# Stage one on rows of x that also come in turned, latents normalised out of PSUM, and a reordered down ring

## Chip, core and metric

One core of a Trainium2 chip runs the whole layer. The metric is the device time of one execution in microseconds. The engines are TensorE (PE, matmuls; PEld is its weight load), VectorE (DVE), ScalarE (ACT), GpSimd (POOL) and SyncE (SP, which here only queues transfers).

## What is computed

One layer on x (1024 x 1024, fp32), shortened:

```python
z = rmsnorm(x, mix_norm_g) @ w_in               # heads of retention, then 448 columns of latents
c_q, c_kv, k_pe = last 448 columns of z         # 256, 128, 64
ret = retention(...)                            # 4 heads
att = mla(rmsnorm(c_q), rmsnorm(c_kv), k_pe)    # 4 heads
x = x + concat(ret, att) @ w_o
h = rmsnorm(x, ffn_norm_g)
x = x + (silu(h @ w_gate) * (h @ w_up)) @ w_down
x = x + sigmoid(rmsnorm(x, ple_norm_g) @ w_ple_gate) * (p @ w_ple_proj)
return rmsnorm(x, final_norm_g)
```

## The kernel before

Each engine runs a program written out by hand; order is kept by semaphores. A full-precision product is three matmuls: every operand is split into a high part (a copy on ScalarE, `..._hi`) and a low part (a subtraction, `..._lo`, on VectorE or POOL), and `product` adds high x high, high x low, low x high over K = 8 slices, 24 matmuls.

Stage one (`sp_1`, `pool_1`, `act_1`, `dve_1`, `pe_1`) makes the latents, tile by tile (T = 8 tiles of 128 tokens). TensorE turns the rows of x (`norm_turn`, L232, 8 transposes), one tile ahead of the product; ScalarE and VectorE split the turned tile out of PSUM (L242, L249) and the weight slices (`mixed_hi` L179, `mixed_lo` L182; the norm's gain is in the weights); ScalarE takes the squares of x (L211) and in `latent_out` the squares of the latents (L335, L336) and their copy, scaled by the row's rstd (L338); VectorE then normalises them in place (`latent_rows`, L413). Two banks of PSUM take the products in turn. The weights of the first retention head come in and are split meanwhile; the angle tables of the rotation are made at tiles 2 and 3. Retention (`pe_2`) starts when all eight copies are done (`ckv_out`).

The down projection's ring (`pe_step`, L1893 to L1895) is one level of a Strassen-like scheme: five chunks of seven steps (35 in all), each 4 x 6 matmuls on a stationary part (hidden rows from DRAM, `sp_rows`, low part by POOL in `rows_lo`, L1871) and a moving part (`w_ffn_down`, `sp_moving`, high part L1859, low part by VectorE in `ring_lo`, L1866). Four of the seven moving parts, T1 to T4, are differences that POOL makes (`moving_sum`: L1833, L1837, L1840, L1845) from four 128 x 1024 slots raw(0) to raw(3). VectorE's program for step s is: two adds of the product to x (L1282), ring_lo of step s+3, two adds. A step may write a bank when the add of an earlier step is done (one to four steps back). SP's program is in one line too: for each u the rows of step u, then moving loads and every four steps a piece of the next stage's weights (`sp_piece`, which waits until the piece before it is split; VectorE splits pieces 2 to 5 between the steps, L182). After the ring `pe_down` (L1936 to L1938) does the last two row blocks with parts made by `down_hi` and `down_lo` (L1920). Stage six turns p on TensorE, two transposes for each of eight tiles (L2237).

## Time and profile before

| | us |
|---|---|
| median of 3 runs | 1295.79 (1295.27 to 1299.84) |
| profiled execution | 1300.8, its span 1299.0 |
| TensorE busy | 1253.7 (97%) |
| VectorE busy | 714.4 (55%) |
| ScalarE busy | 482.7 (37%) |
| GpSimd busy | 486.0 (37%) |

Spans count from the first instruction. A row of a time line has the start, the length, the engine, the line of the kernel, the operation, out<-in, the shape and how many were merged; in brackets the idle time of the engine before it and what ended that. Matmuls overlap, so their pace is the distance of their starts, not their length.

### The profile page before, as it was taken

To read this page: it belongs to the slowest core of one execution; us is meant where nothing else is said; L and a number is where in the kernel's file an instruction comes from. 1 tells how busy PE (TensorE), PEld (TensorE's weight loads), DVE (VectorE), ACT (ScalarE), POOL (GpSimd) and SP (SyncE) were. 2 spreads that over 40 slices of the span, in tenths; PEclk is the share of its full clock that TensorE was granted. 3 is DMA by queue.
4 is the path that set the end of the run, shared out by engine and by line. 5 is a ranking of instruction groups with operands and counts; after the bars stand their busy time and mean duration, and the time that the engine had idled before them with its cause. 6 is when DMAs were issued, how large, how long until landed. Compare 5 with 4: busy or idle time off the path is not lost.

```text
span 1299.0 us, 16923 instructions
## 1 busy us (share of the span) xinstructions
PE 1253.7 (97%) x6052; PEld 1052.9 (81%) x6052; DVE 714.4 (55%) x1193; ACT 482.7 (37%) x889; POOL 486.0 (37%) x502
## 2 busy tenths in 40 slices
PE   7999999989998999999999999999999999999997
PEld 6888888877888888878888888888888778778886
DVE  4634444467556326754444555444489888754433
ACT  5732222246666114533333333333343334314422
POOL 2334444441000002374334555433478777610001
PEclk9999999999999999999999999999999989999999
DMA  6411111010011400133323332332454464330002
GB/s 209 133 34 49 33 50 33 1 41 1 1 65 66 146 1 1 46 109 122 112 83 90 122 111 92 122 102 80 159 212 138 136 211 146 117 110 1 1 33 98
DMA packets 101692, 110.90 MB, mean 85 GB/s; under 512 B 4848, under 2 KB 68720, under 8 KB 101616
## 3 DMA queue, kind: packets, MB, share of 16 engines
q1 hardware_dynamic: 101328, 109.38, 25.8%
q8 instruction: 46, 0.75, 0.2%
q10 hardware_dynamic: 288, 0.52, 0.1%
q14 instruction: 30, 0.25, 0.1%
HBM read 86.29 MB, written 23.59 MB: 85 GB/s over the span
## 4 chain that ended last, share of the span: by engine, by line
PE 74%; issue 9%; POOL 9%; DVE 3%; DMA 2%; ACT 2%; SPq 0%; POOLq 0%; ACTq 0%; DVEq 0%
PE PS L1561 10%; PE PS L1562 10%; PE PS L1563 10%; PE PS L204 4%; PE PS L206 4%; PE PS L205 4%; PE PS L913 3%; PE PS L1893 3%; PE PS L1895 3%; PE PS L1894 3%; PE PS L929 3%; PE PS L2247 2%; PE PS L2245 2%; PE PS L2246 2%; PE PS L708 2%
## 5 line engine op out<-in xcount | busy, mean ns | idle before, releaser
L204 PE MATMUL PS<-WF,HTH 128*128 128x512 f32 (+1 forms) x448 | 177.6, 396 | 2.2 <-ACT X L338 1.5
L206 PE MATMUL PS<-WF,HTL 128*128 128x512 f32 (+1 forms) x448 | 174.0, 388 | 0.0
L205 PE MATMUL PS<-WF,HTH 128*128 128x512 f32 (+1 forms) x448 | 173.7, 388 | 0.0
L1282 DVE TENSOR_TENSOR X<-X,PS 128x512 f32<-128x512 f32 x172 | 110.9, 679 | 79.0 <-PE PS L206 52.7
L1561 PE MATMUL PS<-HTH,WF 128*128 128x512 f32 x336 | 130.7, 389 | 0.0
L1562 PE MATMUL PS<-HTL,WF 128*128 128x512 f32 x336 | 130.7, 389 | 0.0
L1563 PE MATMUL PS<-HTH,WF 128*128 128x512 f32 x336 | 130.7, 389 | 0.0
L1494 DVE TENSOR_TENSOR WF<-RAW,WF 128x512 fp32r<-128x512 f32 x63 | 69.6, 1106 | 81.5 <-ACT WF L1484 81.5
L1561 PE MATMUL PS<-WF 128*128 128x512 f32 x252 | 98.7, 392 | 2.0 <-issue 2.0
L204 PEld LDWEIGHTS PS<-WF,HTH 128*128 128x128 f32 x448 | 84.8, 189 | 17.6 <-ACT X L338 1.9
L1563 PE MATMUL PS<-WF 128*128 128x512 f32 x252 | 98.8, 392 | 0.0
L1562 PE MATMUL PS<-WF 128*128 128x512 f32 x252 | 98.7, 392 | 0.0
L206 PEld LDWEIGHTS PS<-WF,HTL 128*128 128x128 f32 x448 | 84.5, 189 | 16.3
L205 PEld LDWEIGHTS PS<-WF,HTH 128*128 128x128 f32 x448 | 84.8, 189 | 14.9
L1893 PE MATMUL PS<-HTH 128*128 128x512 f32 x200 | 77.8, 389 | 0.0
L1894 PE MATMUL PS<-HTL,HTH 128*128 128x512 f32 x200 | 77.8, 389 | 0.0
L1895 PE MATMUL PS<-HTH,HTL 128*128 128x512 f32 x200 | 77.8, 389 | 0.0
L217 POOL TENSOR_SCALAR ST<-ST 128x1 f32<-128x1 f32 x24 | 5.3, 223 | 189.7 <-ACT HTH L1274 112.6
L561 ACT ACTIVATE TMP<-PS,ST 128x384 f32<-128x384 f32 x32 | 18.6, 580 | 152.5 <-PE PS L206 152.5
L1702 POOL TENSOR_TENSOR TMP<-TMP 128x512 f32<-128x512 f32 x10 | 16.1, 1606 | 157.4 <-DVE TMP L1686 157.4
L1563 PEld LDWEIGHTS PS<-HTH,WF 128*128 128x128 f32 x336 | 63.1, 188 | 13.2
L1561 PEld LDWEIGHTS PS<-HTH,WF 128*128 128x128 f32 x336 | 63.1, 188 | 13.1
(248 smaller groups left out, 2857.6 us busy)
## 6 DMA issues: line engine op xcount, KB each, us to landing
hid<-TMP SPq DMA_DIRECT2D x74, 256.0 KB, 2.3
TMP<-hid SPq DMA_DIRECT2D x25, 512.0 KB, 4.1
RAW<-in_w_ffn_gate SPq DMA_DIRECT2D x22, 512.0 KB, 4.2
RAW<-in_w_ffn_up SPq DMA_DIRECT2D x22, 512.0 KB, 5.5
RAW<-in_w_ffn_down SPq DMA_DIRECT2D x22, 512.0 KB, 5.4
X<-in_x SPq DMA_DIRECT2D x16, 512.0 KB, 4.5
RAW<-in_w_in SPq DMA_DIRECT2D x32, 256.0 KB, 3.2
TAB<-hid SPq DMA_DIRECT2D x9, 512.0 KB, 4.7
```

Of the source, the lines that this page charges most:

```text
L204: nc.tensor.matmul(dst, HTH[:, k, tok], w_h, start=(k == 0), stop=False)
L205: nc.tensor.matmul(dst, HTH[:, k, tok], w_l, start=False, stop=False)
L206: last = nc.tensor.matmul(dst, HTL[:, k, tok], w_h, start=False, stop=(k == K - 1))
L913: last = nc.tensor.matmul(dst, a[:, tok], b[:, blk], start=(i == 0), stop=(i == 4))
L1282: nc.vector.tensor_tensor(x, x, src, ALU.add).then_inc(done, 1)
L1494: nc.vector.tensor_tensor(part(name, 1), part_raw(j, name), part(name, 0).bitcast(F32), ALU.subtract).then_inc(f_w_lo, 1)
L1561: nc.tensor.matmul(dst, w_h, m_h, start=(first and k == 0), stop=False, skip_group_check=True)
L1562: nc.tensor.matmul(dst, w_h, m_l, start=False, stop=False, skip_group_check=True)
L1563: last = nc.tensor.matmul(dst, w_l, m_h, start=False, stop=(k == 3), skip_group_check=True)
L1893: nc.tensor.matmul(dst, h_h, w_h, start=(q < 3 and k == 0), stop=False, skip_group_check=True)
L1894: nc.tensor.matmul(dst, h_h, w_l, start=False, stop=False, skip_group_check=True)
L1895: last = nc.tensor.matmul(dst, h_l, w_h, start=False, stop=(k == 1), skip_group_check=True)
```

## The change

x is also passed in turned (`x_turned`, per tile 128 x 8 x 128), so stage one has no transposes; x itself still comes in, for the squares. Turned tiles lie in six places of X and TMP. The transfer order on SP is new, with the first head's weights in it. All gains come in one load from ScalarE's queue. ScalarE runs one small activation first. TensorE runs 18 products of zeros first. The first weight slices are signalled by halves. Latents stay in PSUM (four banks) until VectorE has scaled and normalised them from there; POOL multiplies the two rstds. The angle tables are at tiles 6 and 7. Retention's first four products wait for the bank they use.

In the ring the moving loads are queued two steps earlier, in another order, and the pieces two steps later; T1 is made in raw(0) instead of T_BUF, after B11's low part, and T2 one step earlier. The four low parts for `pe_down` are made before the last step's adds, in the order 0, 3, 1, 2 (`LAST_ORDER`). p is passed in turned too, and is split from SBUF.

The diff without unchanged and minor lines (eight columns of indent are cut; `...` is what is left out):

```diff
@@ -250,44 +252,82 @@
...
+TURNED_AT = (2048, 3072, 6144, 7168, None, 2048, 3072, None)
+def rows_turned(t):
+    a = TURNED_AT[t]
+    x = tmp(2048, 1024) if a is None else X[:, a:a + 1024]
+    return x.rearrange("p (k n) -> p k n", k=K)
 def sp_1(e):
-    e.dma_start(X3[:, 0, :], t_in["x"][0:P, :]).then_inc(s_x[0], 16)
-    e.dma_start(ident, t_in["table"][:, C_IDENT:C_IDENT + P]).then_inc(s_ident, 16)
-    e.dma_start(GK[:, 0:K], t_in["mix_gain"]).then_inc(s_gk, 16)
-    e.dma_start(GK[:, 2 * K:3 * K], t_in["ple_gain"]).then_inc(s_gk, 16)
     w = t_in["w_in"].rearrange("(k p) n -> p k n", p=P)
-    for m in range(4):
+    def turned(t):
+        if t >= 4:
+            e.wait_ge(s_e[t % 4], 16)
+        if t >= 5:
+            e.wait_ge(n_mix.lo, 10 if t == 7 else 2 * (t - 5) + 2)
+        e.dma_start(rows_turned(t), t_in["x_turned"][t]).then_inc(s_e[t % 4], 16)
+    def rows(t):
+        if t >= 2:
+            e.wait_ge(n_mix.squares, t - 1)
+        e.dma_start(X3[:, t % 2, :], t_in["x"][t * P:(t + 1) * P, :]).then_inc(s_x[t % 4], 16)
+    def weights(m):
...
                     w[:, 2 * m:2 * m + 2, 4 * HALF:4 * HALF + MLA_IN]).then_inc(s_raw[m % 4], 16)
-    for t in range(1, 4):
-        e.dma_start(X3[:, t, :], t_in["x"][t * P:(t + 1) * P, :]).then_inc(s_x[t], 16)
+    turned(0)
+    for m in range(3):
+        weights(m)
+    turned(1)
+    weights(3)
+    rows(0)
+    turned(2)
+    rows(1)
+    turned(3)
...
     e.dma_start(GC[:, QL:QL + KVL], t_in["kv_norm_g"].partition_broadcast(P)).then_inc(s_const, 16)
-    for t in range(4, T):
-        e.wait_ge(n_mix.turned, t - 3)
-        e.wait_ge(n_mix.squares, t - 3)
-        e.dma_start(X3[:, t % 4, :], t_in["x"][t * P:(t + 1) * P, :]).then_inc(s_x[t % 4], 16)
+    turned(4)
+    rows(2)
+    sp_head_weights(e, 0, 0)
+    turned(5)
+    sp_head_weights(e, 0, 1)
+    rows(3)
+    turned(6)
+    sp_head_weights(e, 0, 2)
+    sp_head_weights(e, 0, 3)
+    rows(4)
+    turned(7)
+    rows(5)
+    rows(6)
+    rows(7)
+    e.dma_start(ident, t_in["table"][:, C_IDENT:C_IDENT + P]).then_inc(s_ident, 16)
+IDLE = tmp(3072, P)
 def pool_setup(e):
+    nc.gpsimd.memset(IDLE, 0.0).then_inc(s_setup, 1)
...
     nc.gpsimd.memset(GNE[:, :], GN_EPS).then_inc(s_setup, 1)
-    nc.gpsimd.memset(GK[:, K:2 * K], 1.0).then_inc(s_setup, 1)
...
 def pool_1(e):
...
     def latent_rstd(t):
-        e.wait_ge(ckv_out, 3 * t + 2)
+        e.wait_ge(ckv_out, 2 * t + 2)
...
         e.wait_ge(lat_mean, 2 * t + 2)
-        nc.gpsimd.tensor_tensor(ST[:, 32 + 2 * t:34 + 2 * t], ST[:, 16 + 2 * t:18 + 2 * t], NEGH[:, 0:2],
-                                ALU.pow).then_inc(lat_rstd, 1)
+        c = ST[:, 32 + 2 * t:34 + 2 * t]
+        nc.gpsimd.tensor_tensor(c, ST[:, 16 + 2 * t:18 + 2 * t], NEGH[:, 0:2], ALU.pow).then_inc(lat_rstd, 1)
+        e.wait_ge(lat_rstd, 2 * t + 1)
+        nc.gpsimd.tensor_tensor(c, c, rstd_of(0, t).to_broadcast([P, 2]), ALU.mult).then_inc(lat_rstd, 1)
...
@@ -301,41 +341,57 @@
...
             e.wait_ge(n_mix.squares, t)
-        norm_squares(e, n_mix, t, 0, X3[:, t % 4, :], tmp(0, 1024))
-    e.wait_ge(s_gk, 32)
-    for c in range(4):
+        norm_squares(e, n_mix, t, 0, X3[:, t % 2, :], tmp(0, 1024))
+    def high(t, k=0, n=K):
+        e.wait_ge(s_e[t % 4], 16 * (t // 4 + 1))
+        d = slice(t * P, t * P + P)
+        nc.scalar.copy(HTH[:, k:k + n, d], rows_turned(t)[:, k:k + n]).then_inc(n_mix.hi, n // 4)
+    def slices(c):
         arrived(e, c)
-        mixed_hi(GK, 0, c, raw(c), MLA_IN)
-        if c == 0:
-            turned_hi(e, n_mix, 0)
-    squares(0)
+        for i in range(2):
+            a = c * 1024 + i * HALF
+            gained_hi(WF[:, a:a + MLA_IN], raw(c)[:, i * MLA_IN:(i + 1) * MLA_IN],
+                      GK[:, 2 * c + i:2 * c + i + 1]).then_inc(w_hi if i else w_even_hi, 1)
+    e.dma_start(GK[:, :], t_in["gains"]).then_inc(s_gk, 16)
+    e.wait_ge(s_setup, 4)
+    nc.scalar.activation(ST[:, 120:121], PIH[:, 0:1], ACT.Square).then_inc(s_warm, 1)
+    e.wait_ge(s_gk, 16)
+    high(0, 0, 4)
+    slices(0)
+    high(0, 4, 4)
+    slices(1)
+    slices(2)
+    high(1)
+    slices(3)
     for t in range(T):
-        if t + 1 < T:
-            turned_hi(e, n_mix, t + 1)
-            squares(t + 1)
+        if t + 2 < T:
+            high(t + 2)
+        squares(t)
         if t >= 1:
-            latent_out(e, t - 1)
-        if t >= 4:
-            arrived(e, M_RET + t - 4)
-            e.wait_ge(s_rawb[t - 4], 16)
-            mixed_hi(GK, 1, t - 4, raw(t))
-        if t == 3:
+            latent_squares(e, t - 1)
+        if 3 <= t <= 6:
+            c = t - 3
+            arrived(e, M_RET + c)
+            e.wait_ge(s_rawb[c], 16)
+            mixed_hi(GK, 1, c, raw(c))
+        if t == 7:
...
     e.dma_start(QDEC, t_in["query_decay"]).then_inc(s_const, 16)
-    latent_out(e, T - 1)
-def latent_out(e, t):
+    latent_squares(e, T - 1)
+def latent_squares(e, t):
     e.wait_ge(lat_done, t + 1)
-    b = PS[:, 4 + t % 2]
+    b = PS[:, 4 + t % 4]
     if t:
-        e.wait_ge(ckv_out, 3 * t)
+        e.wait_ge(ckv_out, 2 * t)
...
                          accum_out=ST[:, 17 + 2 * t:18 + 2 * t]).then_inc(ckv_out, 1)
-    nc.scalar.activation(CKV[:, t, 0:MLA_IN], b[:, 0:MLA_IN], ACT.Copy, scale=r).then_inc(ckv_out, 1)
...
@@ -372,26 +428,42 @@
...
 def dve_1(e):
-    def weights_lo(g, c, n=HALF):
-        m = g * M_RET + c
-        e.wait_ge(w_hi, m + 1)
-        mixed_lo(GK, g, c, raw(m), n)
-    for c in range(4):
-        weights_lo(0, c, MLA_IN)
-        if c == 0:
-            turned_lo(e, n_mix, 0)
+    def weights_lo(c):
+        e.wait_ge(w_hi, M_RET + c + 1)
+        mixed_lo(GK, 1, c, raw(c))
+    def low(t, k=0, n=K):
+        e.wait_ge(n_mix.hi, 2 * t + (k + n) // 4)
+        d = slice(t * P, t * P + P)
+        nc.vector.tensor_tensor(HTL[:, k:k + n, d], rows_turned(t)[:, k:k + n], HTH[:, k:k + n, d].bitcast(F32),
+                                ALU.subtract).then_inc(n_mix.lo, n // 4)
+    def slices(c):
+        for i in range(2):
+            a = c * 1024 + i * HALF
+            e.wait_ge(w_hi if i else w_even_hi, c + 1)
+            gained_lo(WF[:, a + 4096:a + 4096 + MLA_IN], raw(c)[:, i * MLA_IN:(i + 1) * MLA_IN],
+                      WF[:, a:a + MLA_IN], GK[:, 2 * c + i:2 * c + i + 1]).then_inc(w_lo if i else w_even_lo, 1)
+    low(0, 0, 4)
+    slices(0)
+    low(0, 4, 4)
+    slices(1)
+    slices(2)
+    low(1)
+    slices(3)
     for t in range(T):
-        if t + 1 < T:
-            turned_lo(e, n_mix, t + 1)
-        if t >= 4:
-            weights_lo(1, t - 4)
-        if t == 2:
+        if t + 2 < T:
+            low(t + 2)
+        if 3 <= t <= 6:
+            weights_lo(t - 3)
+        if t >= 2:
+            latent_rows(e, t - 2)
+        if t == 6:
             tables_dve(e)
-        if t >= 3:
-            latent_rows(e, t - 3)
-    for t in range(T - 3, T):
+    for t in range(T - 2, T):
...
+    e.wait_ge(lat_rows, 3 * T)
...
@@ -406,28 +478,33 @@
 def latent_rows(e, t):
-    e.wait_ge(lat_rstd, t + 1)
-    e.wait_ge(ckv_out, 3 * t + 3)
-    for n, (a, b) in enumerate(((0, QL), (QL, QL + KVL))):
-        c = CKV[:, t, a:b]
-        nc.vector.scalar_tensor_tensor(c, c, ST[:, 32 + 2 * t + n:33 + 2 * t + n], GC[:, a:b],
-                                       ALU.mult, ALU.mult).then_inc(lat_rows, 1)
+    b = PS[:, 4 + t % 4]
+    e.wait_ge(n_mix.rstd, 2 * t + 2)
+    e.wait_ge(ckv_out, 2 * t + 2)
+    nc.vector.tensor_scalar(CKV[:, t, QL + KVL:MLA_IN], b[:, QL + KVL:MLA_IN], rstd_of(0, t), None,
+                            ALU.mult).then_inc(lat_rows, 1)
+    e.wait_ge(lat_rstd, 2 * t + 2)
+    for n, (a, b_end) in enumerate(((0, QL), (QL, QL + KVL))):
+        nc.vector.scalar_tensor_tensor(CKV[:, t, a:b_end], b[:, a:b_end], ST[:, 32 + 2 * t + n:33 + 2 * t + n],
+                                       GC[:, a:b_end], ALU.mult, ALU.mult).then_inc(lat_rows, 1)
+def idle_products(n):
+    for _ in range(n):
+        nc.tensor.matmul(bank(7, P), IDLE, IDLE, start=True, stop=True)
 def pe_1(e):
-    e.wait_ge(s_ident, 16)
-    def turn(t):
-        e.wait_ge(s_x[t % 4], 16 * (t // 4 + 1))
-        norm_turn(e, n_mix, t, X3[:, t % 4, :])
-    turn(0)
+    e.wait_ge(s_setup, 1)
+    idle_products(18)
+    def first(k):
+        if k == 4:
+            e.wait_ge(n_mix.lo, 2)
+        e.wait_ge(w_lo if k % 2 else w_even_lo, k // 2 + 1)
     for t in range(T):
-        if t + 1 < T:
-            turn(t + 1)
-        e.wait_ge(n_mix.lo, 2 * t + 2)
-        if t >= 2:
-            e.wait_ge(ckv_out, 3 * (t - 1))
-        product(bank(4 + t % 2, MLA_IN), t, 0, MLA_IN,
-                (lambda k: e.wait_ge(w_lo, k // 2 + 1)) if t == 0 else None).then_inc(lat_done, 1)
+        e.wait_ge(n_mix.lo, 2 * t + 2 if t else 1)
+        if t >= 4:
+            e.wait_ge(lat_rows, 3 * (t - 3))
+        product(bank(4 + t % 4, MLA_IN), t, 0, MLA_IN, first if t == 0 else None).then_inc(lat_done, 1)
...
@@ -452,15 +529,17 @@
...
+def sp_head_weights(e, h, c):
+    w = t_in["w_in"][:, 0:4 * HALF].rearrange("(k p) (s c) -> p k s c", p=P, s=4)
+    e.wait_ge(w_lo, 4 * h + c + 1)
+    for k in range(2):
+        e.dma_start(RAW[:, c * 1024 + k * HALF:c * 1024 + (k + 1) * HALF].rearrange("p (s c) -> p s c", s=4),
+                    w[:, 2 * c + k, :, h * HD:(h + 1) * HD]).then_inc((s_rawb if k else s_raw)[c], 16)
 def sp_retention(e):
-    w = t_in["w_in"][:, 0:4 * HALF].rearrange("(k p) (s c) -> p k s c", p=P, s=4)
-    with e.Fori(0, HEADS) as h:
+    for h in range(1, HEADS):
         for c in range(4):
-            e.wait_ge(w_lo, M_RET + c - 3 + 4 * h)
-            for k in range(2):
-                e.dma_start(RAW[:, c * 1024 + k * HALF:c * 1024 + (k + 1) * HALF].rearrange("p (s c) -> p s c", s=4),
-                            w[:, 2 * c + k, :, bass.ds(h * HD, HD)]).then_inc((s_rawb if k else s_raw)[c], 16)
+            sp_head_weights(e, h, c)
...
@@ -507,8 +586,10 @@
...
 def pe_2(e):
-    e.wait_ge(ckv_out, 3 * T)
+    e.wait_ge(s_ident, 16)
     for s in range(NR + 3):
+        if s < 4:
+            e.wait_ge(lat_rows, 3 * (5 + s))
...
@@ -1513,15 +1594,15 @@
...
         c, q = u // 7, u % 7
+        if u >= 14 and u % 4 == 2:
+            sp_piece(e, (u - 14) // 4)
...
             sp_moving(e, c + 1, (0,))
-        if c and q == 2:
-            sp_moving(e, c, (1, 3))
-        if c and q == 3:
+        if c and q == 0:
+            sp_moving(e, c, (3, 1))
+        if c and q == 1:
             sp_moving(e, c, (2,))
-        if u >= 12 and u % 4 == 0:
-            sp_piece(e, u // 4 - 3)
-    sp_moving(e, CHUNKS, (1, 3, 2))
+    sp_moving(e, CHUNKS, (3, 1, 2))
...
@@ -1719,13 +1800,14 @@
...
             moving_sum(e, c, 0)
-        if q in (3, 4, 5):
-            moving_sum(e, c, q - 2)
+        if q in MOVING_SUM_AT:
+            moving_sum(e, c, MOVING_SUM_AT[q])
...
+MOVING_SUM_AT = {2: 1, 4: 2, 5: 3}
...
@@ -1775,7 +1857,7 @@
...
         return raw({"B11": 0, "B21": 1, "B22": 3}[name])
-    return raw(2) if name == "T3" else T_BUF
+    return {"T1": raw(0), "T3": raw(2)}.get(name, T_BUF)
...
@@ -1798,8 +1880,8 @@
...
         if c and g == 0:
-            e.wait_ge(r_t, 4 * c - 3)
-            e.wait_ge(d_lo, 7 * c - 6)
+            e.wait_ge(r_t, 4 * c - 2)
+            e.wait_ge(d_lo, 7 * c - 4)
...
@@ -1824,17 +1906,18 @@
 def moving_sum(e, c, n):
     if n == 0:
+        moving_arrived(e, c, 0)
+        moving_arrived(e, c, 2)
+        e.wait_ge(d_lo, 7 * c + 1)
+        nc.gpsimd.tensor_tensor(raw(0), raw(2), raw(0), ALU.subtract).then_inc(r_t, 1)
+    if n == 1:
...
             e.wait_ge(d_lo, 7 * c)
-        moving_arrived(e, c, 0)
-        moving_arrived(e, c, 2)
-        nc.gpsimd.tensor_tensor(T_BUF, raw(2), raw(0), ALU.subtract).then_inc(r_t, 1)
-    if n == 1:
         moving_arrived(e, c, 3)
-        e.wait_ge(d_lo, 7 * c + 3)
-        nc.gpsimd.tensor_tensor(T_BUF, raw(3), T_BUF, ALU.subtract).then_inc(r_t, 1)
+        e.wait_ge(r_t, 4 * c + 1)
+        nc.gpsimd.tensor_tensor(T_BUF, raw(3), raw(0), ALU.subtract).then_inc(r_t, 1)
...
@@ -1926,7 +2011,7 @@
...
             if n < 4:
-                e.wait_ge(f_added, N_DOWN - 2 + n if n < 2 else N_DOWN)
+                e.wait_ge(f_added, N_DOWN - 1 if n == 0 else N_DOWN)
...
@@ -1976,22 +2061,24 @@
...
             ring_lo(e, s + 3)
+        elif s < STEPS - 1:
+            down_lo(e, LAST_ORDER[s + 3 - STEPS])
...
             piece_lo(e, (s - 10) // 4)
-        if s >= 31:
-            down_lo(e, s - 31)
-s_p, p_turned, p_hi, p_lo = sem("s_p"), sem("p_turned"), sem("p_hi"), sem("p_lo")
-s_e = [sem(f"s_e{i}") for i in range(4)]
+        if s == STEPS - 2:
+            down_lo(e, LAST_ORDER[2])
+            down_lo(e, LAST_ORDER[3])
+s_p, p_hi, p_lo = sem("s_p"), sem("p_hi"), sem("p_lo")
...
 PW = 16384
-PIN = tmp(0, 2048).rearrange("p (t n) -> p t n", t=T)
+PIN = tmp(0, 2048).rearrange("p (k n) -> p k n", k=2)
...
@@ -2085,15 +2172,15 @@
 def p_part(t, y):
...
-def p_bank(t):
-    return PS[:, 5 + 2 * (t % 2), 0:2 * P].rearrange("p (k n) -> p k n", k=2)
+def p_rows(t):
+    return PIN[:, :, t * P:t * P + P]
 def act_6(e):
     def p_high(t):
-        e.wait_ge(p_turned, t + 1)
         if t == 0:
+            e.wait_ge(s_p, 16)
             e.wait_ge(f_down, N_DOWN + 2 * T)
-        nc.scalar.copy(p_part(t, 0), p_bank(t)).then_inc(p_hi, 1)
+        nc.scalar.copy(p_part(t, 0), p_rows(t)).then_inc(p_hi, 1)
...
@@ -2233,9 +2319,6 @@
...
         if half == 0:
-            for k in range(2):
-                last = nc.tensor.transpose(PS[:, 5 + 2 * (u % 2), k * P:k * P + P], PIN[:, t, k * P:k * P + P], ident)
-            last.then_inc(p_turned, 1)
...
```

## Rows read from the trace of the kernel before

**Rows 1.** The page, first part: busy time, share of the span, instructions.
```profile
PE 1253.7 (97%) x6052; PEld 1052.9 (81%) x6052; DVE 714.4 (55%) x1193; ACT 482.7 (37%) x889; POOL 486.0 (37%) x502
```
**Rows 2.** TensorE's waits, whole span: who waited for whom, us, times, longest.
```profile
PE PS L1893 <- DVE X L1282: 7.1, 3, 3.0
...
PE PS L1936 <- DVE WF L1920: 1.9, 1, 1.9
```
**Rows 3.** Time line of TensorE in stage one.
```profile
11.71 1.97 PE L232 MATMUL PS<-CST,X 128*128 128x128 f32 x8 [5.13 <-DMA X<-in_x]
13.33 0.72 PE L204 MATMUL PS<-WF,HTH 128*128 128x448 f32 x1
...
20.05 1.03 PE L232 MATMUL PS<-CST,X 128*128 128x128 f32 x8
20.84 0.45 PE L204 MATMUL PS<-WF,HTH 128*128 128x448 f32 x1
...
25.79 1.03 PE L232 MATMUL PS<-CST,X 128*128 128x128 f32 x8
...
61.04 0.50 PE L204 MATMUL PS<-WF,HTH 128*128 128x512 f32 x1 [1.53 <-ACT X L338]
```
**Rows 4.** Time lines of SP, ScalarE and VectorE at the front.
```profile
2.59 1.97 SPq L260 DMA_DIRECT2D RAW<-in_w_in  x4
...
6.94 1.28 ACT L179 ACT_TABLE_LOAD   x1 [6.94 <-DMA RAW<-in_w_in]
...
11.89 3.66 DVE L182 SCALAR_TENSOR_TENSOR WF<-RAW,GK,WF 128x448 fp32r<-128x448 f32 x6
```
**Rows 5.** The tile RAW, first 16 us: its four loads.
```profile
DMA to landing us min/median/max: 4.3/5.3/6.3
```
**Rows 6.** Stretches: length, busy PE, PEld, DVE, ACT, POOL, clock, DMA share, GB/s.
```profile
12.00:14.00 2.00, 2.00 (x10) 1.96 (x9) 2.00 (x4) 2.00 (x5) 0.00 (x0) 1.00 1.01 398
...
45.00:50.00 5.00, 5.00 (x30) 4.65 (x29) 2.83 (x6) 3.93 (x11) 1.82 (x5) 1.00 0.38 108
```
**Rows 7.** VectorE by line and form in the ring: busy us, mean ns.
```profile
L1920 DVE TENSOR_TENSOR WF<-RAW,WF 128x1024 fp32r<-128x1024 f32 x4 | 4.9, 1215 | 0.0
```
**Rows 8.** The ring as one stretch.
```profile
944.64:1150.20 205.56, 196.46 (x841) 160.22 (x840) 174.63 (x186) 73.75 (x78) 146.73 (x54) 0.98 0.45 156
```
**Rows 9.** Time line of TensorE in the ring.
```profile
982.90 0.39 PE L1893 MATMUL PS<-HTH 128*128 128x512 f32 x1
...
988.35 0.39 PE L1893 MATMUL PS<-WF 128*128 128x512 f32 x1
...
1036.64 0.50 PE L1893 MATMUL PS<-WF 128*128 128x512 f32 x1 [1.44 <-DVE X L1282]
...
1058.95 0.77 PE L1893 MATMUL PS<-WF 128*128 128x512 f32 x1 [2.96 <-DVE X L1282]
...
1063.78 0.63 PE L1895 MATMUL PS<-WF 128*128 128x512 f32 x1
...
1108.31 0.47 PE L1893 MATMUL PS<-WF 128*128 128x512 f32 x1 [2.72 <-DVE X L1282]
...
1150.20 0.71 PE L1936 MATMUL PS<-WF 128*128 128x512 f32 x1 [1.91 <-DVE WF L1920]
```
**Rows 10.** Waits of POOL and of SP's queue in the ring.
```profile
POOL TMP L1833 <- DMA RAW<-in_w_ffn_down: 22.5, 4, 6.8
...
SPq L2054 <- DVE WF L182: 34.1, 3, 15.7
```
**Rows 11.** Time lines of POOL and VectorE in the ring.
```profile
1032.52 2.39 POOL L1840 TENSOR_TENSOR RAW<-RAW 128x1024 f32<-128x1024 f32 x1
1032.59 3.40 DVE L1866 TENSOR_TENSOR HTL<-RAW,HTH 128x1024 fp32r<-128x1024 f32 x1
...
1041.61 2.47 DVE L1282 TENSOR_TENSOR X<-X,PS 128x512 f32<-128x512 f32 x4
```
**Rows 12.** TensorE by line and form, stage six.
```profile
L2237 PE MATMUL PS<-CST,TMP 128*128 128x128 f32 x16 | 3.0, 272 | 0.0
```

27 lines of the change are left out of this document (16 added, 11 removed).

## The prediction

> **What bounds the kernel now.** I read the page's first part, then TensorE's waits, then time lines of the two places where these waits lie. TensorE's matmuls are busy for 97% of the span [rows 1], so time can come only from fewer instructions on TensorE, from its waits, or from stretches at half clock. The longest sums of waits are in the down stage: 7.1 us at L1893 for adds on VectorE, and 1.9 us at L1936 [rows 2]. The other place is the front. The second block of transposes waits 5.13 us for x, the first product starts at 13.33, and retention starts at 61.04 after a last wait of 1.53 us for ScalarE's copy of the latents [rows 3].
>
> The profiled execution took 1300.8 us for a span of 1299.0, 5.0 us over the median of 1295.79. The sum is made against the former; at the end I come back to the difference.
>
> **Part 1, the front.** Product 0 ends at 20.05; behind it come seven products of 4.95 us (20.84 to 25.79), 34.6 in all, and six blocks of eight transposes at 0.79 us (20.05 to 20.84), 4.7 in all, so product 7 ends at 59.4, and 1.7 us with the wait of 1.53 in them lie before 61.04 [rows 3]. Stage one's transposes go, since rows of x come in turned. This takes 6 x 0.79 = 4.7 us off the path, and the wait for the copy (1.7 us) goes too: retention's first product needs only the latents of tile 4, out of a bank that was done 3 products before.
>
> What is left is the start of product 1: 20.84 before. Now it comes when the low part of the last weight slice is there. Loads: before, x's first rows, three small loads and the first weights, 1.06 MB, had landed at 2.59 + 4.3 = 6.9 us, the last weights at about 4.1 + 6.3 = 10.4; the rate with a full queue is 398 GB/s [rows 4 to 6]. After, only turned tile 0 stands ahead of the weights, at 1.18 instead of 2.59. I place the first slice at 5.8 (between 5.4, if the 0.46 MB follow the first load at 398 GB/s, and 6.8), each next at +1.2, the last at 10.7 with turned tile 1 between. The table load of 1.28 us that ScalarE did after the first landing [rows 4] is brought forward by the warm-up activation and hidden by the load. VectorE is the slow one: half-slice of weights 0.61 (3.66 us for six [rows 4]), a turned tile 1.2 (as the 1024 columns at L1920, 1215 ns [rows 7]). From 6.4, when ScalarE has its first half: eight half-slices 4.9, the second half of tile 0 0.6, tile 1 1.2, half a microsecond of gaps: the last is done at 13.4 and the product at 14.0 us. Seven products without transposes, 7 x 4.90 = 34.3, end at 48.3. So retention starts at 48.3 instead of 61.04: **-12.7 us**. The range is -9.5 (loads at the late bound, no ScalarE lead, half clock through product 0 and 1) to -14.
>
> What hides the rest: ScalarE per tile does a copy, squares, latent squares and a weight pair; it was busy 3.93 of 5 us with the latent copy in it, which goes [rows 6]. VectorE gets three reads of PSUM per tile in place of two of SBUF; it has 2.83 of 5 us [rows 6]. Four banks in turn instead of two give these reads three products of room. SP now queues 11.2 MB before turned tile 7; at 398 GB/s that is done at about 31 us, and product 7 needs it at 43. rows(t) waits for the squares of t-2, and turned tiles, head weights stand behind it on SP, but tiles are asked for two products ahead. The angle tables move to tile 6 on VectorE (nine operations), and behind them the last latents wait, so VectorE comes to retention's first tile about when TensorE has finished the second projection: 0 to 2 us of new wait there; I take 0.
>
> The 18 zero products are costed at nothing: eight transposes at 0.23 us apart (11.71, x8, 1.97 us [rows 3]) make about 4 us for 18, which end before the weights are there. Their worth is the clock: product 0 took 6.72 us (13.33 to 20.05) against 4.95 for a later one, since its first ten matmuls ran at the 1.2 GHz spacing; after, it is paced by VectorE anyway, so a clock that stays low costs 0.5 us, bounds 0 and 2.
>
> **Part 2, the down ring.** 35 steps took 205.56 us (944.64 to 1150.20); an undisturbed step is 5.45 (982.90 to 988.35), 35 of them 190.7. So 14.9 us are lost: 1.44 + 2.96 + 2.72 + 1.91 us of waits, and 5.9 around them, most of it half clock: behind the waits of 2.96 and of 2.72 matmuls start 0.43 apart instead of 0.23 (row at 1063.78) [rows 8, 9]. The last wait (1.91) also lowers the clock in the part behind the ring: another 1.6, priced like the row at 1108.31.
>
> Cause: POOL waits 22.5 us for moving rows in four chunk starts, and SP stood 34.1 us at the piece loads waiting for VectorE [rows 10], with the moving and row loads queued behind. POOL's sums come late, ScalarE and ring_lo behind them, and the adds stand behind ring_lo in VectorE's program. The change asks for the moving rows two steps earlier, and for the pieces two later, when the buffer is nearly free; T2 is a step earlier too. T1 now goes into the slot of B11 and waits for B11's low part, which VectorE does at step 7c-3; ring_lo of T1 is due at 7c-1, two steps or 10.9 us later, against 2.4 for the sum and 1.05 for the copy. POOL then waits for VectorE there, with rows_lo of the next steps queued behind, but they are due later still. So I expect the DMA waits to go and nothing as long in their place. At the end the four low parts come before the last step's adds instead of one behind them, so the 1.91 goes as well. I leave 1.5 us of small waits: -14.9 - 1.6 + 1.5 = **-15.0 us**, range -17 to -7.
>
> What speaks against it: VectorE's SBUF reads collide with POOL. A low part takes 1.2 us alone [rows 7] but 3.40 beside POOL's sum at 1032.52 (2.39). With four adds in a row (2.47 [rows 11]) that makes 5.7 to 5.9 a step, more than TensorE's 5.45; POOL's waits were what let VectorE catch up. POOL needs 11 x 2.39 a chunk, two per such cycle, so 5.5 of 7 steps are of the long kind and the chunk takes VectorE 37 of 38.1 us; in the chunk with three pieces it overruns by some 3 us, against 4 us of room before an add is late.
> The Trainium skill (SBUF — State Buffer, "SBUF: two separate sides") says the pair of ports that VectorE and GpSimd share is an exclusive lock, and that an operation with two SBUF inputs blocks fully against one of GpSimd that reads SBUF; the rows agree (1.2 plus a whole 2.4 is 3.6), and by that rule a POOL that never waits is no free gain but takes VectorE over the step, which is rival 1.
>
> **Part 3, p.** p comes in turned: 16 transposes of stage six go. At 0.11 us apart (eight in 0.79 with the change-over [rows 3]; x16, 272 ns each with the pipeline [rows 12]) that is **-1.8 us**. The splits now read SBUF instead of PSUM, and have no due time before the gate product's 24 matmuls end.
>
> Sum: -12.7 - 15.0 - 1.8 = -29.5; 1300.8 - 29.5 = 1271.3. Against the median of 1295.79 it would be 1266.3. Part of the 5.0 between them is probably waits and half clock of the ring, which go anyway; I take the middle: **1268.5 us**.
>
> **Rivals.**
> 1. The ring becomes bound by VectorE and POOL's shared port: 35 steps of 5.71 us (1.21 + two POOL operations of 2.39 less overlap) are 199.9, 9.2 over the ideal. For it: 3.40 at 1032.59. Against: POOL needs only 11 of 14 places. Time 1268.5 + 7.7 = 1276.
> 2. The ring keeps its loss, with POOL waiting for B11's low part instead of the DMA: 1268.5 + 15.0 = 1283.5. Against: the 10.9 us of room.
> 3. The front gains only the transposes (the slices come as late as before): 1268.5 + 6.5 = 1275.
> 4. Slower: x now comes in twice, and stage one waits for its loads. It decides if the 11.2 MB take longer than 43 us; to lose all, retention would have to start 16.8 us later than before, turned tile 7 at 73, a rate under 160 GB/s. At 140 it is 1305. Against it 398 GB/s [rows 6].
> 5. The order on SP does not do what it says: pieces still block. Then as 2.
>
> **Numbers.** Chances: forecast 0.66, rival 1 0.15, rivals 2 and 5 0.07, rival 3 0.09, rival 4 0.03. The range goes from 1260 (both parts at their good ends) to 1284, which takes in rivals 1 to 3. A measurement of this kernel can tell about 0.5%, 6.5 us, from no change; every case but the fourth gains more, so faster 0.95, same 0.03, slower 0.02.
>
> **What would show it.** Right: product 1 at 14 us, no transposes up to the first head, retention at 48; POOL's wait at T1 no longer for a DMA; the ring 192 to 194 us, no half clock in it; the down part starting under 0.3 us after the ring. Wrong: a wait for x's turned rows in stage one; ring steps of 5.7; a wait for low parts of T1; TensorE waiting for VectorE just after the first retention product.

## The result, and the profile after

The changed kernel takes 1276.19 us (median of four runs, 1275.8 to 1279.47) against 1296.69 for the kernel before, run beside it: a ratio of 0.9843, 95% interval 0.9823 to 0.9863, 20.5 us less. The forecast of 1268.5 was 27.3 under the median of before that it knew (1295.79), so the changed kernel came in 7.7 over it and inside the range of 1260 to 1284. The profiled execution took 1279.47 us, with a span of 1277.7, 21.3 less than before's 1299.0. The readings below are of that execution. A granted clock of 1.00 is TensorE's full 2.4 GHz, 0.50 is the half clock of 1.2 GHz, and a value between is the mean of a stretch that has both.

The page's first part, which answers to [rows 1], and TensorE's waits over the whole span (engine and line that waits, who is waited for, us, times, longest), which answer to [rows 2]:

```profile
PE 1245.1 (97%) x6008; PEld 1046.6 (82%) x6008; DVE 730.6 (57%) x1194; ACT 480.3 (38%) x875; POOL 495.1 (39%) x510
```

```profile
PE PS L994 <- ACT TMP L1035: 4.2, 4, 1.1
PE PS L1976 <- DVE X L1363: 3.4, 4, 1.5
PE PS L1642 <- issue: 2.9, 1, 2.9
...
PE PS L607 <- POOL TMP L673: 2.1, 2, 1.9
```

The ring's waits for adds (L1976 for L1363, in before L1893 for L1282) fell from 7.1 to 3.4 us, and the wait behind the ring is gone. A new one stands at L607: 1.9 us for POOL, in the first head of retention.

The time line of TensorE in stage one, which answers to [rows 3] (start, length, engine and line, operation, idle time before it and its releaser):

```profile
12.80 0.47 PE L206 MATMUL PS<-WF,HTH 128*128 128x448 f32 x1 [0.95 <-DVE WF L184]
...
14.13 0.37 PE L206 MATMUL PS<-WF,HTH 128*128 128x448 f32 x1
...
48.65 0.39 PE L206 MATMUL PS<-WF,HTH 128*128 128x512 f32 x1
...
61.60 0.36 PE L607 MATMUL PS<-CST,TMP 128*128 128x128 f32 x1 [1.89 <-POOL TMP L673]
61.83 0.78 PE L206 MATMUL PS<-WF,HTH 128*128 128x512 f32 x1
```

Product 1 starts at 14.13 in place of 20.84, held up by the low parts of the weights, and retention at 48.65 in place of 61.04. Then comes the wait, and the matmul behind it takes 0.78 us in place of 0.39. The stretches of the changed kernel (length, busy us of PE, PEld, DVE, ACT, POOL, granted clock, DMA share, GB/s): ten microseconds with that wait in them, the ring, the part up to the gate stage, and the rest.

```profile
60.00:70.00 10.00, 8.40 (x33) 6.88 (x34) 2.50 (x5) 1.79 (x6) 3.27 (x6) 0.83 0.19 53
...
937.25:1132.43 195.18, 191.79 (x841) 157.31 (x840) 188.38 (x186) 74.57 (x78) 150.34 (x54) 1.00 0.49 166
1132.43:1156.81 24.38, 24.38 (x122) 20.42 (x120) 12.69 (x19) 9.01 (x16) 5.20 (x14) 1.00 0.26 100
1156.81:1277.70 120.89, 113.62 (x523) 94.14 (x521) 49.01 (x73) 39.39 (x82) 8.26 (x19) 0.98 0.09 35
```

So the span's 21.3 us divide as follows. Retention starts 12.4 earlier; 5.0 of that are lost again by the ring's start (944.64 to 937.25, 7.4 ahead), 3.6 of them within three products of retention. The ring is 10.4 shorter [rows 8], at full clock throughout. The part behind it is 1.9 shorter (26.32 to 24.38), and the rest 1.6 (122.5 to 120.9).

What is left in the ring, on TensorE (answering to [rows 9]), on VectorE and among POOL's waits there (answering to [rows 10]):

```profile
1047.63 0.47 PE L1976 MATMUL PS<-WF 128*128 128x512 f32 x1 [1.42 <-DVE X L1363]
1050.86 0.50 PE L1976 MATMUL PS<-WF 128*128 128x512 f32 x1 [0.27 <-DVE X L1363]
1093.70 0.47 PE L1976 MATMUL PS<-WF 128*128 128x512 f32 x1 [1.47 <-DVE X L1363]
1096.94 0.50 PE L1976 MATMUL PS<-WF 128*128 128x512 f32 x1 [0.23 <-DVE X L1363]
```

```profile
1042.07 4.82 DVE L184 SCALAR_TENSOR_TENSOR WF<-GB,GK,WF 128x512 fp32r<-128x512 f32 x2
...
1088.45 4.50 DVE L184 SCALAR_TENSOR_TENSOR WF<-GB,GK,WF 128x512 fp32r<-128x512 f32 x2
```

```profile
POOL RAW L1912 <- DVE WF L1949: 13.1, 2, 8.3
POOL RAW L1912 <- DVE HTL L1949: 6.2, 2, 4.8
```

POOL still waits 19.3 us at the four chunk starts, now for VectorE's low part of B11. TensorE's two groups of waits begin some 4 us behind the start of the two pairs of low parts of pieces at 1042.07 and 1088.45, and their first wait ends 5.2 to 5.6 us behind it. Of 34 intervals between steps 29 are the undisturbed 5.44 us. Steps 19 to 21 take 7.02, 6.08 and 5.72, steps 27 and 28 7.07 and 6.09.

### The profile page after: what moved, and what is told of

It is laid out like the page before. It is cut to its first block, busy times and chain, and to the rows that moved or that the text cites. A ratio compares the mean times of both kernels' runs of the same rounds, so it can differ in the third digit from the quotient of the medians.

```text
span 1277.7 us, 16752 instructions
## 1 busy us (share of the span) xinstructions
PE 1245.1 (97%) x6008; PEld 1046.6 (82%) x6008; DVE 730.6 (57%) x1194; ACT 480.3 (38%) x875; POOL 495.1 (39%) x510
## 4 chain that ended last, share of the span: by engine, by line
PE 85%; issue 5%; DVE 4%; POOL 2%; DMA 2%; ACT 2%; SPq 0%; POOLq 0%; ACTq 0%; DVEq 0%
PE PS L1644 10%; PE PS L1642 10%; PE PS L1643 10%; PE PS L206 6%; PE PS L208 6%; PE PS L207 6%; PE PS L1976 4%; PE PS L1977 4%; PE PS L1978 4%; PE PS L994 3%; PE PS L1010 3%; PE PS L2328 2%; PE PS L2330 2%; PE PS L2329 2%; PE PS L789 2%
## 5 line engine op out<-in xcount | busy, mean ns | idle before, releaser
L1363 DVE TENSOR_TENSOR X<-X,PS 128x512 f32<-128x512 f32 x172 | 109.9, 677 | 67.4 <-PE PS L208 52.6
L1642 PE MATMUL PS<-HTH,WF 128*128 128x512 f32 x336 | 131.0, 390 | 0.0
L1642 PE MATMUL PS<-WF 128*128 128x512 f32 x252 | 98.6, 391 | 2.9 <-issue 2.9
L1976 PE MATMUL PS<-HTH 128*128 128x512 f32 x200 | 77.9, 390 | 0.0
L1643 PEld LDWEIGHTS PS<-HTL,WF 128*128 128x128 f32 x336 | 63.2, 188 | 13.3
L1642 PEld LDWEIGHTS PS<-HTH,WF 128*128 128x128 f32 x336 | 63.2, 188 | 13.1
```

The costliest lines, as they stand in the source:

```text
L1363: nc.vector.tensor_tensor(x, x, src, ALU.add).then_inc(done, 1)
L1642: nc.tensor.matmul(dst, w_h, m_h, start=(first and k == 0), stop=False, skip_group_check=True)
L1643: nc.tensor.matmul(dst, w_h, m_l, start=False, stop=False, skip_group_check=True)
L1976: nc.tensor.matmul(dst, h_h, w_h, start=(q < 3 and k == 0), stop=False, skip_group_check=True)
```

## The experiments

Three questions: where the 3.6 us go behind 48.65, which part of the ring's edit brought its 10.4, and what the ring's remaining 4.7 us (195.18 less 35 x 5.44) are. All kernels start from the changed one. "Retention" is the start of its first product, "to 4th" from there to the fourth; the last two columns come from the start times of TensorE in the profiled execution.

| kernel | median us | ratio to before (95%) | retention | to 4th | ring | behind it |
|---|---|---|---|---|---|---|
| before | 1296.69 | | 61.04 | 17.07 | 205.56 | 26.32 |
| changed | 1276.19 | 0.9843 (0.9823 to 0.9863) | 48.65 | 20.68 | 195.18 | 24.38 |
| changed again | 1278.54 | 0.9851 (0.9826 to 0.9876) | 48.84 | 20.74 | 195.16 | 24.38 |
| 1 old ring | 1289.56 | 0.9939 (0.9920 to 0.9957) | 48.84 | 18.93 | 205.14 | 26.12 |
| 2 tables early | 1276.18 | 0.9837 (0.9804 to 0.9870) | 49.74 | 16.99 | 195.13 | 24.37 |
| 3 no zero products | 1275.06 | 0.9831 (0.9801 to 0.9860) | 48.87 | 19.14 | 195.12 | 24.38 |
| 4 pieces small | 1275.16 | 0.9828 (0.9798 to 0.9857) | 49.01 | 20.72 | 192.62 | 24.38 |
| 5 order of loads alone | 1277.16 | 0.9841 (0.9809 to 0.9872) | 48.95 | 20.78 | 194.36 | 24.45 |
| 6 sums alone | 1284.05 | 0.9900 (0.9869 to 0.9931) | 48.55 | 19.13 | 200.64 | 24.39 |
| 7 front order | 1274.54 | 0.9829 (0.9807 to 0.9851) | 49.08 | 17.00 | 195.11 | 24.37 |
| 8 front and pieces | 1269.32 | 0.9789 (0.9765 to 0.9814) | 48.95 | 16.96 | 191.02 | 24.38 |
| 8 again | 1270.74 | 0.9803 (0.9784 to 0.9822) | 49.78 | 16.99 | 191.08 | 24.38 |
| 10 less is enough | 1269.79 | 0.9794 (0.9780 to 0.9807) | 48.59 | 16.98 | 192.16 | 24.38 |

The ring's column repeats to 0.1 us among the kernels with the ring of the changed one; the old ring is 205.56 in before and 205.14 in kernel 1. The stretch from the fourth product to the ring's start, in which nothing was edited, varies from 864.6 to 869.0. Much of that is TensorE's clock. Two stretches of the changed kernel (867.9 from the fourth product to the ring), then the same of kernel 7 (864.6):

```profile
260.00:280.00 20.00, 14.82 (x86) 12.68 (x85) 15.48 (x45) 7.95 (x17) 8.23 (x20) 0.83 0.12 45
550.00:560.00 10.00, 7.99 (x28) 6.46 (x29) 5.31 (x7) 2.11 (x5) 7.22 (x6) 0.83 0.27 102
```

```profile
260.00:280.00 20.00, 15.26 (x94) 13.12 (x95) 17.33 (x46) 8.93 (x18) 8.67 (x20) 0.91 0.00 1
550.00:560.00 10.00, 10.00 (x46) 8.28 (x45) 5.68 (x6) 3.56 (x6) 9.68 (x7) 1.00 0.76 235
```

A mean granted clock of 0.83 over 20 and over 10 us loses 3.4 and 1.7 us (an estimate from these rows: the missing share times the length), 5.1 in all; kernel 7 loses 1.8. That is the 3.3 us between the two. In before the clock is 0.94 over 260 to 290 and 0.91 over 550 to 570, some 3.6 us. TensorE's wait at L1642 near 550 differs too, from 1.80 (kernel 3) to 3.38 us (kernel 1). So differences of 1 to 4 us are read from the traces here, and not from the medians.

**1. The old ring.** Order of loads, sums and order of the last four low parts as before.

```diff
-                if u >= 14 and u % 4 == 2:
-                    sp_piece(e, (u - 14) // 4)
...
-                if c and q == 0:
-                    sp_moving(e, c, (3, 1))
-                if c and q == 1:
+                if c and q == 2:
+                    sp_moving(e, c, (1, 3))
+                if c and q == 3:
                     sp_moving(e, c, (2,))
+                if u >= 12 and u % 4 == 0:
+                    sp_piece(e, u // 4 - 3)
...
-        MOVING_SUM_AT = {2: 1, 4: 2, 5: 3}
...
-        LAST_ORDER = (0, 3, 1, 2)
+        LAST_ORDER = (0, 1, 2, 3)
```

> The changed kernel with its down ring put back as before: the order of the ring's transfers, the four moving sums with T1 in T_BUF, and the order of the last four low parts. Stage one and p keep the change. Theory: the ring edits alone took the ring from 205.56 to 195.18 us and what follows it up to the gate stage from 26.32 to 24.38, so this kernel is 10.4 + 1.9 = 12.3 us slower than the changed one (ratio 1.0096), its ring is at 205 to 206 us again, and its stage one stays where the changed kernel has it. Rival: part of the 10.4 us came with the earlier start of the ring (7.4 us) and with other placing of transfers in it; then the ring is at 198 to 203 here and the kernel only 5 to 9 us slower.

Measured: 13.4 us over the changed kernel by the medians (11.0 over its repetition, 12.4 by the difference of the two ratios to before), and 11.7 from the ring's start to the gate stage. The stretches ring and behind it, POOL's wait, and one row of TensorE:

```profile
934.23:1139.37 205.14, 195.60 (x841) 158.61 (x839) 174.67 (x186) 73.77 (x78) 146.93 (x54) 0.98 0.45 156
1139.37:1165.49 26.12, 26.12 (x120) 21.66 (x121) 12.02 (x18) 9.02 (x16) 5.18 (x14) 0.93 0.29 101
```

```profile
POOL TMP L1914 <- DMA RAW<-in_w_ffn_down: 21.8, 4, 7.8
```

```profile
1096.49 0.76 PE L1974 MATMUL PS<-WF 128*128 128x512 f32 x1 [4.74 <-DVE X L1363]
```

The DMA waits and the lower clock are back. The ring's gain is its own and owes nothing to its earlier start. About 2 us of it belong to the new order of the last four low parts: the last step takes 7.52 us here and in before, and 5.44 in the changed kernel.

**5 and 6. The two halves of that edit.** Kernel 5 keeps the new order of loads and takes the sums of before; kernel 6 keeps the new sums (below) and takes the order of before. Both keep the new end of the ring.

```diff
             if n == 0:
-                moving_arrived(e, c, 0)
-                moving_arrived(e, c, 2)
-                e.wait_ge(d_lo, 7 * c + 1)
-                nc.gpsimd.tensor_tensor(raw(0), raw(2), raw(0), ALU.subtract).then_inc(r_t, 1)
-            if n == 1:
                 if c == 0:
...
+                moving_arrived(e, c, 0)
+                moving_arrived(e, c, 2)
+                nc.gpsimd.tensor_tensor(T_BUF, raw(2), raw(0), ALU.subtract).then_inc(r_t, 1)
+            if n == 1:
                 moving_arrived(e, c, 3)
-                e.wait_ge(r_t, 4 * c + 1)
-                nc.gpsimd.tensor_tensor(T_BUF, raw(3), raw(0), ALU.subtract).then_inc(r_t, 1)
+                e.wait_ge(d_lo, 7 * c + 3)
+                nc.gpsimd.tensor_tensor(T_BUF, raw(3), T_BUF, ALU.subtract).then_inc(r_t, 1)
...
```

> The changed kernel with the moving sums of before (T1 and T2 in T_BUF, VectorE's low part of T1 between them) and their waits, but the changed order of the ring's loads (the loads of the second and third raw buffers a step or two earlier, the pieces behind u = 14, 18, ...). Theory L (the loads): what the ring lost in before was POOL's wait for its loads, because they stood behind the pieces in SP's queue; then this kernel has no DMA waits of POOL over 3 us in all, its ring is 195 to 198 us, and it is 0 to 3 us slower than the changed one. Theory S (the sums): the chain T1, its low part, T2 through one buffer sets the ring; then POOL's 22 us of waits turn into waits for VectorE's low part, and the ring stays at 202 to 206, the kernel 7 to 11 slower than the changed one.

> The changed kernel with the order of the ring's loads as before, and the changed moving sums (T1 in the first raw buffer). The other half of the same question. Theory L: POOL waits for its loads as in before (about 20 us), the ring is at 202 to 206 us, and the kernel 7 to 11 us slower than the changed one. Theory S: 195 to 198 us and 0 to 3 us slower. If both halves alone stay near 195 to 198, either is enough; if both are at 202 to 206, it takes the two together.

The ring of either as a stretch, each with POOL's longest waits in it, kernel 5 first:

```profile
938.72:1133.08 194.36, 191.92 (x842) 157.17 (x840) 171.36 (x186) 73.78 (x78) 148.49 (x54) 1.00 0.49 165
```

```profile
POOL TMP L1918 <- DVE HTL L1947: 15.6, 3, 6.1
...
POOL TMP L1914 <- DMA RAW<-in_w_ffn_down: 1.7, 2, 1.4
```

Kernel 6:

```profile
934.27:1134.91 200.64, 194.04 (x841) 158.68 (x840) 179.86 (x186) 73.97 (x78) 150.90 (x54) 0.98 0.47 161
```

```profile
POOL RAW L1912 <- DMA RAW<-in_w_ffn_down: 23.9, 4, 7.9
```

With the loads early and the old sums the ring is at 194.36, even 0.8 under the changed kernel. With the new sums and the old order POOL waits 23.9 us for loads, and TensorE once 5.10. So the loads' order carries what the new end does not, 8 to 9 us against kernel 1. Kernel 6 is nearer to the changed one than either theory said (5.5 us): its ring is 4.5 us under kernel 1's, some 2 by the new end and 2.4 by the sums, so moving the sums softens the loss where the loads are late. As expected for theory S, POOL's waits in kernel 5 turned into waits for VectorE (15.6 us). They cost 1.3 us (steps 2 and 6 take 5.65 and 6.53), less than the old sums save at steps 27 and 28. The name of the releaser does not tell whether a wait matters; its place in the step does.

The edit of the loads has two parts, moving loads earlier and pieces later, and no kernel takes them apart. The trace of before tells that a piece ahead of them in SP's queue is not the whole cause. At its first chunk start no piece has been queued yet (the first is at 981.20):

```profile
967.99 0.37 SPq L1795 DMA_DIRECT2D TMP<-hid  x1
968.40 0.47 SPq L1813 DMA_DIRECT2D RAW<-in_w_ffn_down  x1
```

```profile
975.01 2.40 POOL L1833 TENSOR_TENSOR TMP<-RAW 128x1024 f32<-128x1024 f32 x1 [3.69 <-DMA RAW<-in_w_ffn_down]
```

POOL waits 3.69 us for the moving load of 968.40, which SP issued at once behind the rows of its step (967.99), and SP issues those rows only when POOL is done with an earlier row part. The load's place in the program is too late by itself. At the second and fourth start (6.53 and 6.81 us) a piece does stand in front.

**4. The pieces made small.** The low parts of pieces 2 to 5 are one column wide.

```diff
+                w = 1 if z < 6 else HALF
-                last = gained_lo(WF[:, b + n:b + n + HALF], piece_raw(z)[:, i * HALF:i * HALF + HALF], WF[:, b:b + HALF],
+                last = gained_lo(WF[:, b + n:b + n + w], piece_raw(z)[:, i * HALF:i * HALF + w], WF[:, b:b + w],
```

> The changed kernel in which the low parts of pieces 2 to 5 (w_ple_gate) are made of one column in place of 512, both halves: most of those low parts is left out, and the output lacks them. Theory A (VectorE beside POOL): the ring's residue of 195.2 - 190.5 = 4.7 us comes from these four operations of two each on VectorE, which take 4.5 to 4.8 us a pair beside POOL against 1.4 alone, and delay the adds of the ring at steps 19 to 21 and 27 to 28; without them the ring is at 191 to 192 us and the kernel 3 to 4.5 us faster (ratio 0.9965 to 0.998). Theory B: the residue comes from POOL's wait for the low part of B11 that the change added for T1 (13.1 and 6.2 us); it does not go with the pieces, and the ring stays at 194 to 195.5.

The ring is 192.62, 2.6 under the changed kernel, less than the 3 to 4 of theory A. Why only half goes is in one row of VectorE:

```profile
1040.87 3.83 DVE L184 SCALAR_TENSOR_TENSOR WF<-GB,GK,WF 128x1 fp32r<-128x1 f32 x2
```

Two operations on one column each still hold VectorE for 3.83 us. POOL works without a gap there, in the same trace:

```profile
1039.92 2.40 POOL L1912 TENSOR_TENSOR RAW<-RAW 128x1024 f32<-128x1024 f32 x1 [4.78 <-DVE HTL L1949]
1042.28 2.40 POOL L1954 TENSOR_TENSOR WF<-TMP,WF 128x1024 fp32r<-128x1024 f32 x1
1044.64 2.40 POOL L1920 TENSOR_TENSOR TMP<-RAW 128x1024 f32<-128x1024 f32 x1
```

VectorE's first operation, of 1.47 us, ends at 1042.34 and its second, of 2.44, at 1044.70; POOL's end at 1042.32 and 1044.68. So most of the price of such an operation beside POOL is not its size: it waits for POOL's current operation to end, and two in a row wait twice. POOL pays too: in the changed kernel the operation at L1954 between the two full-sized low parts takes 2.87 us in place of 2.40. The Trainium skill (SBUF — State Buffer, "SBUF: two separate sides") says that whichever operation starts first holds the shared pair of ports for its whole length, and that the other fully blocks. These rows agree.

**2 and 7. The tables of angles.** Kernel 2 puts them back to t=2 and t=3. Kernel 7 also puts the latent rows ahead of the weights' low parts. The part of kernel 7's edit on VectorE (ScalarE's half of the tables moves from t=7 to t=3 in both):

```diff
+                if t >= 2:
+                    latent_rows(e, t - 2)
                 if 3 <= t <= 6:
                     weights_lo(t - 3)
-                if t >= 2:
-                    latent_rows(e, t - 2)
-                if t == 6:
+                if t == 2:
                     tables_dve(e)
```

> The changed kernel with the tables of angles computed where they were before, on VectorE after the rows of t=2 and on ScalarE at t=3, in place of t=6 and t=7. Theory A: the 3.6 us that the front loses between the first and the fourth retention product come from the tables: VectorE has them in 46.7 to 51.9, ScalarE waits 5.32 us for them, and so squares, rstd, rows, rope and rotation of the last block all end about 5 us late, TensorE waits 1.89 us at 61.60 and runs at a lower granted clock from 60 to 70. Then the wait goes, the clock is at full, and the kernel is 3.6 us faster (3 to 4; ratio 0.9972). Theory B: the low clock does not hang on the wait, then only 1.9 us go. Theory C: the last block's chain is late in any case, because the four products of the rotation and the copies on POOL (59.86 to 61.55) set it; then nothing changes, or the tables now hold up the stage's products in the middle and the first retention product comes 1 to 3 us later.

> The changed kernel with two moves on VectorE in stage one: the tables of angles at t=2 (ScalarE's half at t=3), and the latent rows of a block ahead of the low parts of the retention weights in the same turn. Theory: product 6 waits for the PSUM bank that the rows of block 2 give back, and those rows stood behind a low part that waits for ScalarE; with the two moves product 6 loses nothing (it lost 0.7 to 0.8 us, and 1.1 with the tables early alone), the first retention product starts at 48.0 to 48.3, and the wait of 1.9 us at 61.6 and the half clock that sometimes follows it are gone: 2.5 to 3 us less than the changed kernel, up to 4.5 against an execution with the half clock (ratio to it 0.998). Rival: the rows wait for POOL's rstd and the squares behind the loads of x, whatever stands ahead of them; then product 6 stays late by 0.7 to 1.1 and the gain is 1 us.

In the changed kernel, on VectorE and ScalarE, the tables stand ahead of the last block's work:

```profile
46.69 0.16 DVE L411 CAST POSF<-POS 128x8 f32<-128x8 int32 x1
...
51.17 0.69 DVE L419 SCALAR_TENSOR_TENSOR TMP<-TAB 128x512 f32<-128x512 f32 x1
...
55.72 0.74 DVE L488 SCALAR_TENSOR_TENSOR X<-PS,ST,GC 128x256 f32<-128x256 f32 x2 [1.25 <-POOL ST L330]
```

```profile
51.89 0.63 ACT L426 ACTIVATE TAB<-TAB 128x512 f32<-128x512 f32 x1 [5.32 <-DVE TMP L419]
```

ScalarE waits 5.32 us for them with the squares of the last block behind it; rstd, rows, rope and rotation follow, and POOL's part ends at 61.55. With the tables early the wait at L607 is gone in both kernels, and the half clock with it (kernel 7):

```profile
60.00:70.00 10.00, 10.00 (x48) 8.32 (x47) 3.71 (x9) 3.44 (x8) 3.11 (x7) 1.00 0.18 52
```

The fourth product comes 16.99 and 17.00 us behind the first, as in before (17.07), in place of 20.7. Theory A holds for the wait. But kernel 2 pays 0.9 us ahead of it, as the second half of theory C said, and its median shows no gain (1276.18 against 1276.19): product 6 starts at 39.75 in place of 38.8 to 39.2. It waits for the PSUM bank of block 2, that is for its latent rows, and the tables delay these. My remedy in kernel 7 (the rows ahead of the low parts) gave back at most what kernel 2 had lost. The rows now wait for POOL's rstd, as the rival said:

```profile
38.20 0.74 DVE L488 SCALAR_TENSOR_TENSOR X<-PS,ST,GC 128x256 f32<-128x256 f32 x2 [2.13 <-POOL ST L330]
```

Kernel 7's own start of retention, 49.08, is no gain over 48.84. In time it is 4.0 us under the repetition of the changed kernel, with intervals that overlap; the trace carries this verdict.

**3. No zero products.**

```diff
-            idle_products(18)
+            idle_products(0)
```

> The changed kernel without the 18 zero products (36 instructions, 7.21 us on TensorE) that stand ahead of the first product. Theory by the forecast's step: TensorE starts its first product at full clock only because of them; without them the first products run at half clock, at most the 4.96 us of one product again over the time until the clock rises, less what the loads hold up anyway; I take 1 to 3 us slower. Rival: the first product waits for its slices of the weights in any case, so nothing is lost: within 0.5 us.

```profile
7.20 0.71 PE L206 MATMUL PS<-WF,HTH 128*128 128x448 f32 x1 [7.20 <-DVE WF L184]
7.71 0.57 PE L207 MATMUL PS<-WF,HTH 128*128 128x448 f32 x1
...
12.78 0.37 PE L206 MATMUL PS<-WF,HTH 128*128 128x448 f32 x1
...
14.61 0.36 PE L206 MATMUL PS<-WF,HTH 128*128 128x448 f32 x1
...
39.07 0.44 PE L206 MATMUL PS<-WF,HTH 128*128 128x448 f32 x1
```

The matmuls of product 0 now start 0.37 us apart up to 12.5, the spacing of 1.2 GHz, in place of 0.20 (the profile's granted clock reads 1.00 there all the same). Yet product 1 starts only 0.5 to 0.8 us later than in kernels 1, 2 and 4 (13.83 to 14.09), since the changed kernel waits for weights there. Product 6 starts at 39.07, where it stood with them (38.85 to 39.21), and retention at 48.87. The 0.5 to 0.8 us are waited for again at product 6. They are worth nothing here.

**The changed kernel again, and 8: pieces divided.** Kernel 8 is kernel 7 with one of a piece's two operations at step s and the other at s + 2.

```diff
-                    piece_lo(e, (s - 10) // 4)
+                    piece_lo(e, (s - 10) // 4, (0,))
+                if s >= 20 and s % 4 == 0 and s <= 32:
+                    piece_lo(e, (s - 12) // 4, (1,))
...
```

> The changed kernel itself, beside the next two on the same chip, so that differences of 1 to 3 us between them can be read: ratio to before 0.984 as measured (1274 to 1277 us), first retention product at 48.6 to 49.0, a wait of 1.7 to 2.0 us for POOL at 61 to 62, product 6 held up by 0.7 to 0.8 us where the products run 4.86 us apart, ring 195.1 to 195.2 us.

> As the kernel with the two moves in stage one, and the low parts of pieces 2 to 5 on VectorE in the ring divided: the first 512 columns at step s, the others two steps later, in place of both in one step. Theory: a pair costs VectorE 4.5 to 4.8 us in one step of 5.44, which already holds about 4.9 of other work, so the adds fall behind by more than the PSUM banks cover; divided, the same work lies over three steps, the two waits of 1.4 us on TensorE shrink to 0.3 or less, and the ring is at 192.5 to 193.5 us in place of 195.2: another 2 us less. Rival: VectorE is at 188 of 195 us whatever the order, so the delay only moves to a later step: ring 194.5 to 195.5.

The repetition of the changed kernel took 1278.54 us, a little over what was expected; its milestones came as expected. In kernel 8, the ring as a stretch, and one of the divided operations:

```profile
931.27:1122.29 191.02, 190.70 (x842) 157.60 (x840) 183.72 (x186) 74.55 (x78) 152.73 (x54) 1.00 0.50 169
```

```profile
1036.01 2.00 DVE L184 SCALAR_TENSOR_TENSOR WF<-GB,GK,WF 128x512 fp32r<-128x512 f32 x1
```

The ring is 191.02, 0.6 over 35 undisturbed steps, better than the 192.5 expected. VectorE does the same work and is busy 4.7 us less: the eight low parts of pieces take 12.0 us in sum, in place of 16.3, because the second of a pair took 2.88 to 2.89 us in the changed kernel, and a part alone takes 1.68 to 2.00, or 0.74 where POOL is idle (two of eight here, one there). TensorE's only wait there is 0.3 us. The kernel takes 1269.32 us, 9.2 less than the changed one beside it, where I expected 4.5 to 5. Between their profiled executions lie 10.3: 4.1 are the ring, 3.7 the front, and the rest is in the stretch between, which is 2.5 us shorter (867.8 to 865.4) without an edit in it.

**10, and 8 again.** Kernel 8 with the sums of before and no zero products.

> The kernel with the two moves in stage one and the divided pieces (1269.3 us; ratio 0.979), less two parts of the change: the moving sums are those of before (T1 and T2 in T_BUF), and there are no zero products at the front. Theory: neither bought anything. The ring's gain was the order of its loads (with the old sums alone it was 194.4 us against 195.2), and what the zero products give product 1 (0.5 to 0.8 us) is waited for again at product 6. Then this kernel is within 1 us of the other, its ring 190.8 to 192.5 us, its first retention product within 0.3 us of 48.9. Rival: once the pieces no longer hold VectorE up, the chain T1, low part, T2 through one buffer shows at steps 2 and 6 (5.65 and 6.52 us there with the old sums); then the ring is 193 to 195 and the kernel 2 to 3 us slower.

> The kernel with the two moves in stage one and the divided pieces once more, beside the other on one chip: ratio to before 0.979 again (0.977 to 0.981), ring 191.0 us, no wait at 61 us, first retention product 48.9.

```profile
930.22:1122.38 192.16, 191.15 (x841) 157.42 (x840) 168.69 (x185) 74.09 (x78) 149.62 (x54) 1.00 0.49 168
```

The medians are the same within their spread (1269.79 and 1270.74). The zero products are worth nothing here either. The sums show 1.1 us in the ring (1.1 at step 6, 0.2 to 0.4 at steps 2 and 26, against 0.6 at one step of kernel 8), half of what the rival said. Both kernels are faster than the changed one, about 0.5%, and than the one before, 2.0 to 2.1%.

## Why the prediction was right, and where it was off

**Front, -12.7: right at its milestones, -12.4.** Product 1 came at 14.13 (forecast 14.0), retention at 48.65 (48.3). The pace came from VectorE's low parts, as said. The terms of that sum in the forecast give 13.6, not 13.4, for the last low part, which changes nothing. The 18 zero products were costed at about 4 us and took 7.21, two instructions each (x36); product 0 starts at 7.95 behind them, at 7.20 without them (kernel 3) and at 7.12 in kernel 2 with them, so they still cost nothing. In the profiled execution of the changed kernel six products ran 4.96 us apart. In kernels 1, 4, 5, 6 and the repetition they ran 4.86 apart and retention still started at 48.6 to 49.0, because product 6 came 0.4 to 1.0 us late, for the latent rows of block 2. I had given the four banks "three products of room"; they are at their limit.

**"0 to 2 us of new wait there; I take 0": the step that failed.** The forecast named the tables at tile 6 with the last latents behind them, and then took the low end. It was 1.89 us, at the rotation in the first head, and 1.95 in most other executions. TensorE waiting just behind the first retention product was one of the forecast's own signs of being wrong; it waits for POOL and not for VectorE. And the forecast left out what such a wait can do to the clock. The profiled executions with this wait are seven: in four of them (the changed kernel twice, 4, 5) the fourth product comes 20.7 us behind the first, with a granted clock of 0.83 in 60 to 70; in three (1, 3, 6) 18.9 to 19.1 at full clock. So the term was 1.9, or 3.7 with the half clock.

**Ring, -15.0: -10.4 and -1.9.** That the moving loads came too late was the right cause, and kernels 1, 5 and 6 show it. That the pieces ahead of them were what held them up is shown in part only: the first of POOL's four waits has no piece in front. That T1's new place was needed was not: it is worth nothing in the changed kernel and 1.1 us once the pieces are divided. "Nothing as long in their place" was wrong by the row: POOL waits 19.3 us for VectorE. It was right by the reason given, the room of two steps. The mis-sized term is "1.5 us of small waits", which is 4.7. I weighed the pieces in sum ("overruns by some 3 us, against 4 us of room"), as if VectorE's work beside POOL could be added up. The price is a wait for POOL's operation, once per operation, and a pair in one step paid it twice: 4.8 us in one step of 5.44. Kernel 8, with the pair divided, has 0.6 left of the 4.7. The end of the ring came as forecast: the down part starts 0.2 us after it, at full clock.

**p, -1.8: about right.** The part from the gate stage to the end is 1.6 us shorter. No kernel takes this part, or the front as a whole, out alone; both are read from the milestones.

**Sum.** Against the profiled execution, 1271.3 were forecast and 1279.5 came: 8.2 more. 5.0 were lost between retention's start and the ring (3.6 the tables' wait with its clock, 1.4 in the stretch up to the ring, where by the granted clocks above the changed kernel loses 5.1 us and before 3.6). 2.7 are the ring with its end, and 0.5 the rest of the front and p. The choice between profile and median made little difference: the changed kernel's profiled execution is also 3.3 us over its median. The middle of 1271.3 and 1266.3 is 1268.8, not 1268.5.

**Rivals.** Rival 1 gave the time that came, 1276, but this is chance: more than half of what the forecast missed lies ahead of the ring, and in the ring steps of 5.71 throughout were not seen, 29 of 34 are at 5.44. Its mechanism acts only where a step has one operation more. Rivals 2, 3 and 5 fell with the time lines. Of rival 4 there is a trace: ScalarE waits for rows of x in stage one, 2.02 us for a turned tile in kernel 8 and 2.76 in its repetition, where products 5 and 6 come later for the latent rows and retention starts at 49.78 in place of 48.95. That is about 1 us, not the 30 it would need.

## What to carry over

Where a queue issues loads for two users, ask which of its waits comes earliest in the program and what stands behind it, and how late the load itself stands; the new order of the loads and pieces brought 8 to 9 us, the new sums nothing. Where VectorE works beside a GpSimd that never rests, price an operation by what is left of GpSimd's current one, not by its columns alone, and keep two that contend out of one step. When a step's cost is bounded as "0 to 2, I take 0", and the work behind it has been moved later on purpose, take the upper half, and add what TensorE's clock may do behind the wait.

## What the runs showed of the hardware

Two VectorE operations of one column each took 3.83 us beside GpSimd operations of 2.40 (kernel 4), and each ended with one of them. One of 512 columns took 0.74 us while GpSimd was idle, 1.7 to 2.0 alone in a step of kernel 8, and once 2.89 in kernel 10, where it began 0.05 us behind one of GpSimd's: what is left of GpSimd's operation sets it.

The same wait of 1.73 to 1.96 us on TensorE was followed by a half clock in four executions of seven. Nothing in the code decides it: six of the seven have the same code up to there. Its price, about 1.7 us, is as large as the wait itself. The same holds farther on: a wait of 2.47 us at 273.70 has the half clock around it in the changed kernel (granted clock 0.83 from 270 to 280), and at 270.47 in kernel 7 it has none (1.00).
